# One block of tokens is normed, queried and chosen ahead of the others; the norms of the last two blocks stand behind the first products of fetched rows

## The reference

```python
o = jnp.concatenate([o_gdn, o_rwkv], axis=-1) @ w_out[layer]
x = x + gt1 * o[:, n_ctx:]
x = x + gt2 * peer_ffn(modulate(rms_norm(x, norm2_g[layer]), sh2, sc2), ...)

def peer_ffn(h, w_query, sub_keys, down, up):
    q = (h @ w_query).reshape(B, T, PEER_HEADS, 2, PEER_DKEY // 2)
    s = jnp.einsum('bthpd,hpkd->bthpk', q, sub_keys).astype(jnp.float32)
    s_top, i_top = lax.top_k(s, PEER_TOPK)
    ...
    best_s, pos = lax.top_k(cand_s, PEER_TOPK)
    idx = jnp.take_along_axis(cand_i, pos, axis=-1)
    gate = jax.nn.softmax(best_s, axis=-1)
    ...
        act = jax.nn.gelu(jnp.einsum('td,ted->te', h_blk, down[i_blk]), approximate=False)
        return jnp.einsum('te,ted->td', act * g_blk, up[i_blk])
```

## Time and profile before

| | us |
|---|---|
| median of 3 runs | 4005.07 (4001.75 to 4008.58) |
| the profiled execution's own time | 4012.65 |
| its span, first to last instruction | 4010.8 |
| TensorE busy in the span | 3541.0 (88%) |
| VectorE busy | 2607.9 (65%) |
| ScalarE busy | 1024.8 (26%) |
| GpSimd busy | 1212.8 (30%) |

### The profile page before, as it was taken

The page is one execution under the profiler, slowest core; times in us unless marked ns, Lnnn a source line. Parts: engine busy times, 40 slices in busy tenths (PEclk is TensorE's granted clock), DMA queues, the critical chain, the costliest instruction groups (busy, mean ns, idle before and its releaser), DMA issues. The chain is left out here.

```text
span 4010.8 us, 54734 instructions
## 1 busy us (share of the span) xinstructions
PE 3541.0 (88%) x21607; PEld 2096.7 (52%) x21607; DVE 2607.9 (65%) x4972; ACT 1024.8 (26%) x2744; POOL 1212.8 (30%) x1197
## 2 busy tenths in 40 slices
PE   7998899999987988777777777689999999999998
PEld 4556666888845544332233333355555444458863
DVE  4866535787656666776777675556666667547765
ACT  1432222444222323323333333330000012510000
POOL 1034301544211334333333334223232320014432
PEclk8999999999998999999999999999999999999999
DMA  4157620000028999999999999701112431012233
GB/s 173 42 211 244 229 76 1 11 3 3 3 95 296 402 416 420 420 421 420 420 420 421 420 421 420 305 23 46 60 63 95 167 131 64 1 42 85 85 135 137
DMA packets 184398, 786.68 MB, mean 196 GB/s; under 512 B 13574, under 2 KB 76305, under 8 KB 109136
## 3 DMA queue, kind: packets, MB, share of 16 engines
q0 software_dynamic: 77408, 550.32, 33.3%
q1 hardware_dynamic: 105584, 230.77, 16.4%
q10 hardware_dynamic: 1152, 2.10, 0.1%
HBM read 781.03 MB, written 2.10 MB: 195 GB/s over the span
## 5 line engine op out<-in xcount | busy, mean ns | idle before, releaser
L2584 PE MATMUL bank<-row,dg 128*128 128x512 f32 x1444 | 699.3, 625 | 207.6 <-ACT dg L2693 207.2
L2786 DVE CUSTOM_DVE_ANT_0 row<-row,bank 128x1024 f32<-128x1024 f32 x361 | 440.9, 1221 | 297.1 <-DMA row<-in_experts,idxs 276.9
L2584 PEld LDWEIGHTS bank<-row,dg 128*128 128x128 f32 x1444 | 275.4, 198 | 595.7 <-issue 582.8
L2852 POOL DMA_INDIRECT row<-in_experts,idxs x361 | 348.6, 966 | 627.3 <-PE bank L2584 565.7
L2584 PE MATMUL bank<-wring,dg 128*128 128x512 f32 x604 | 288.1, 610 | 71.2 <-ACT dg L2693 71.2
L104 PE MATMUL bank<-hT,wring 128*128 128x256 f32 (+1 forms) x864 | 285.1, 490 | 3.7 <-ACT sq L830 3.0
L3548 DVE TENSOR_TENSOR pad<-pad,bank 128x256 f32<-128x256 f32 (+2 forms) x396 | 154.1, 412 | 191.9 <-PE bank L104 184.6
L2684 ACT ACTIVATE act<-dots 128x2 f32<-128x2 f32 x256 | 52.0, 203 | 825.2 <-DVE dots L2786 825.2
L2786 DVE CUSTOM_DVE_ANT_0 wring<-wring,bank 128x1024 f32<-128x1024 f32 x151 | 184.5, 1222 | 111.3 <-DMA wring<-in_experts,idxs 103.3
L2584 PEld LDWEIGHTS bank<-wring,dg 128*128 128x128 f32 x604 | 112.8, 194 | 230.9 <-issue 223.8
L104 PEld LDWEIGHTS bank<-hT,wring 128*128 128x128 f32 x864 | 165.4, 192 | 118.8 <-issue 101.3
(11 more groups left out here) (605 smaller groups left out, 6591.6 us busy)
## 6 DMA issues: line engine op xcount, KB each, us to landing
wring<-in_ada_w SPq DMA_DIRECT2D x64, 1024.0 KB, 5.6
wring<-in_ffn_w_down SPq DMA_DIRECT2D x50, 1024.0 KB, 6.9
wring<-in_ffn_w_up SPq DMA_DIRECT2D x44, 1024.0 KB, 7.7
wring<-in_peer_w_query SPq DMA_DIRECT2D x16, 1024.0 KB, 10.9
wring<-in_w_in SPq DMA_DIRECT2D x7, 2048.0 KB, 8.3
wring<-in_ada_w SPq DMA_DIRECT2D x4, 2048.0 KB, 11.1
wring<-in_attn_w_qkv SPq DMA_DIRECT2D x3, 2048.0 KB, 7.9
row<-in_experts,idxs POOLq DMA_INDIRECT x361, 24.7
```

What stands on the lines that cost most here:

```text
L2584: ins = e.matmul(ks[half], self.dg[u % 4], self.places[self.slot[u]][:, 1024 + half * 512:1536 + half * 512], start=(x == 0), stop=(x == 127))
L2786: e.tensor_tensor_reduce(row, row, P.pairs[g % 2], 1.0, 0.0, MUL, ADD, self.dots[:, g % 2, x:x + 1]).then_inc(*V.up("pg_dot", j))
L2852: e.indirect_dma_start(self.places[r], None, P.i["experts"], bass.IndirectOffsetOnAxis(ap=idu[:, b, j % 128:j % 128 + 1], axis=0)).then_in ...
```

## The change

`Experts` loses its `super().pe(pe)` and the like, and what `Experts` did ahead of the 512 steps moves into `MixerOut`.

- TensorE: the keys are turned right behind block 2's turn; behind the products of blocks 3 and 2 come the turn of block 3's `h2`, queries 0 to 7 with their scores, then the four `out_pe` of blocks 1 and 0 (first the half f whose weights lie in ring slot 0, then the other, 1-f; here f = 1), then queries 8 to 15, the gate row, and the turns of `h2` of blocks 2, 1, 0.
- ScalarE: its work is put in the matching order. `weigh` of block 3 stands ahead of queries 8 to 15; the roots of blocks 2, 1, 0 stand among those queries.
- VectorE: `heads_dv` of block 0 behind `normed(3)`; the choice of block 3; `normed(1)` behind the dot of row 0, `normed(0)` behind that of row 1, the gate row behind that of row 2.
- SyncE: the first eight query tiles go through two places (where `sk` lay and where `ogdn` lay) where there were four; each waits for the tile two ahead of it.
- GpSimd: the first seven fetches wait for what lies in their places: `wfree` for j = 0 to 2, the queries of tile 6 for j = 3, `pq_rows` of block 0 (the end of `normed(0)`) for j = 4 to 6. `final_norm_g` is loaded ahead of j = 8.

```diff
@@ MixerOut.dv
             self.heads_dv(dv, b)
         self.added(dv, 3, 0)
         self.added(dv, 3, 1)
-        self.heads_dv(dv, 0)
         dv.wait_ge(*P.at("pq_scale"))
         e.tensor_scalar(self.Ar, self.Ar, 1.0, None, ADD).then_inc(*V.up())
-        self.added(dv, 2, 0)
-        self.added(dv, 2, 1)
...
         self.normed(dv, 3)
+        self.heads_dv(dv, 0)
+        self.added(dv, 2, 0)
+        self.added(dv, 2, 1)
+        choice, f = P.experts.choose(dv, 3, 0), self.first
+        take(choice, 10)
+        self.added(dv, 1, f)
+        take(choice, 2)
+        self.added(dv, 0, f)
+        take(choice, 1)
+        self.added(dv, 1, 1 - f)
+        for _ in choice:
+            pass
+        self.added(dv, 0, 1 - f)
         self.normed(dv, 2)
-        self.added(dv, 1, 0)
-        self.added(dv, 0, 0)
-        self.added(dv, 1, 1)
-        self.normed(dv, 1)
-        self.added(dv, 0, 1)
-        self.normed(dv, 0)
@@ MixerOut.ac
+        ac.wait_ge(*P.at("ro_y", 0))
+        for n in range(8):
+            x.query_ac(ac, 0, n)
+            if n:
+                x.scores_ac(ac, 0, n - 1)
+            if n == 3:
+                self.squares(ac, 2)
+        self.turned_ac(ac, 0, 1)
+        x.scores_ac(ac, 0, 7)
+        x.rows_ac(ac, 0)
+        x.weigh(ac, 3, 0)
+        self.squares(ac, 1)
+        for n in range(8, 16):
+            x.query_ac(ac, 0, n)
+            if n > 8:
+                x.scores_ac(ac, 0, n - 1)
+            if n == 10:
+                self.squares(ac, 0)
+                self.root(ac, 2)
+            if n == 12:
+                self.root(ac, 1)
+            if n == 14:
+                self.root(ac, 0)
+        x.scores_ac(ac, 0, 15)
+        for b in (2, 1, 0):
+            self.out_ac(ac, b)
@@ MixerOut.pe
+        self.out_pe(pe, ws, 2, 0)
+        self.heads_pe(pe, 1)
+        self.gate_pe(pe, 0)
+        self.out_pe(pe, ws, 2, 1)
+        P.cycle((2, 3, 4, 5))
+        self.rows_pe(pe, 3)
+        pe.wait_ge(*P.at("free", "pq_h", 3, 1))
+        pe.wait_ge(*P.at("free", "pq_keys", 3))
+        for n in range(8):
+            x.query_pe(pe, 0, n, 0, 8)
+            if n:
+                x.scores_pe(pe, 0, n - 1)
+        P.cycle((6, 7, 0, 1))
+        self.heads_pe(pe, 0)
+        k = P.own(pe, 2, "pq_s", 0, 7)
+        x.scores_pe(pe, 0, 7, k)
+        self.out_pe(pe, ws, 1, f)
+        self.out_pe(pe, ws, 0, f)
+        T_.mark("wfree", ws[f][0])
+        self.out_pe(pe, ws, 1, 1 - f)
+        self.out_pe(pe, ws, 0, 1 - f)
+        T_.mark("wfree", ws[1 - f][0])
+        P.cycle((2, 3, 6, 7))
+        for n in range(8, 16):
+            x.query_pe(pe, 0, n, 0, 8)
+            if n > 8:
+                x.scores_pe(pe, 0, n - 1)
+        x.scores_pe(pe, 0, 15)
+        mod_row(pe, P, T_, "pg_gate", lambda n: P.modT[0][:, 40 + n, 0:1])
         for b in (2, 1, 0):
             self.rows_pe(pe, b)
@@ Experts.dv
+            if j == 0:
+                P.rout.normed(dv, 1)
+            if j == 1:
+                P.rout.normed(dv, 0)
+            if j == 2:
+                keep_row(dv, P, V, "pg_gate", self.gt)
@@ Experts.po
-            elif r >= early - 2:
-                po.wait_ge(*P.at("query_w_free", 4 + r - (early - 2)))
+            elif r >= 4:
+                po.wait_ge(*P.at("pq_rows", 0))
+            elif r == 3:
+                po.wait_ge(*P.at("query_w_free", 6))
+            else:
+                po.wait_ge(*P.at("wfree", ws[f if r < 2 else 1 - f][0]))
```

More of the change, by code:

```diff
@@ L1669, in __init__ @@
         self.bon = P.mem("bon", 2048, 4, 4, 128)
+        self.ybase = P.top
         self.y = P.mem("y", 2048, 4, 8, 64)
@@ L2144, in __init__ @@
         assert P.top <= hbase + 27 * T
+        P.top = hbase + 27 * T
+        self.oT = [P.mem("oT", 2048, 4, NX)]
+        assert P.top <= rs.ybase
+        P.top = hbase + 11 * T + 4096
+        self.oT.append(P.mem("oT", 2048, 4, NX))
+        assert P.top <= hbase + 19 * T
         P.top = rs.big
@@ L2277, in ac @@
         A.mark("ro_bs")
+        x = P.experts
         for b in self.BLOCKS:
@@ L2296, in ac @@
             e.activation(self.skT[:, 4 * q:4 * q + 4, :], v4(P.ps("pq_keys", q)), ACT.Copy).then_inc(*A.up("free", "pq_keys", q))
-        self.out_ac(ac, 2)
-        self.squares(ac, 0)
-        self.root(ac, 0)
-        self.out_ac(ac, 1)
-        self.out_ac(ac, 0)
+        self.squares(ac, 3)
+        self.root(ac, 3)
+        self.turned_ac(ac, 1, 1)
+        self.root_ac(ac, 0)
+        self.out_ac(ac, 3)
+        ac.wait_ge(*P.at("ro_y", 0))
[24 more added lines that the diff above has]
+            self.out_ac(ac, b)
     def root_ac(self, ac, b):
@@ L2346, in pe @@
         ws = [P.weight("pe", 8, 512) for _ in range(2)]
+        x, f = P.experts, ws[0][0] % 2
+        self.first, self.ws = f, ws
         self.heads_pe(pe, 3)
@@ L2394, in out_pe @@
         pe.wait_ge(*P.at("free", "ro_T", b, 1))
-        mm(pe.e, k, [(self.oT[:, c, b * 128:(b + 1) * 128], wb[:, c, :]) for c in range(8)]).then_inc(*self.T.up("ro_o", half, b))
+        mm(pe.e, k, [(self.oT[c // 4][:, c % 4, b * 128:(b + 1) * 128], wb[:, c, :]) for c in range(8)]).then_inc(*self.T.up("ro_o", half, b))
     def rows_pe(self, pe, b):
@@ L2492, in __init__ @@
         quarter = [P.wring[:, n * 2048:(n + 1) * 2048] for n in range(4)]
-        self.wq = Tiles(P, "query_w", quarter, 8)
-        first += quarter[0:2]
+        P.top = P.obase
+        self.wq = Tiles(P, "query_w", quarter[2:4] + [first[0], P.mem("wq", 2048)], 8)
+        first = quarter[0:2] + [first[1], first[0]] + first[2:]
         self.places = first + old + quarter[2:4] + hq
@@ L2519, in place @@
     def place(self, n):
-        return n % 4 if n < 8 else 2 + n % 2
+        return 2 + n % 2 if n < 8 else n % 2
     def sy(self, sy):
@@ L2525, in sy @@
         wq = P.i["peer_w_query"][0].rearrange("(c p) n -> p c n", p=128)
-        P.begin(sy, "rout")
         for n in range(16):
-            after = None if n < 4 else n - 4 if n < 8 else 6 + n % 2 if n < 10 else n - 2
+            after = None if n < 2 or n in (8, 9) else n - 2
+            if n == 0:
+                sy.wait_ge(*P.at("pq_keys", 3))
+            if n == 1:
+                sy.wait_ge(*P.at("ro_T", 0, 0))
+            if n == 8:
+                sy.wait_ge(*P.at("wfree", P.rout.ws[1 - P.rout.first][0]))
             self.wq.load(sy, n, self.place(n), after, wq[:, :, n % 8 * 256:n % 8 * 256 + 256])
@@ L2536, in query_pe @@
         if c0 == 0:
+            if which and n == 0:
+                pe.wait_ge(*P.at("free", "pq_h", 0, 1))
             self.kq = P.bank(pe, "pq_q", which, n)
@@ L2545, in query_pe, with scores_pe @@
                 self.T.mark("query_w_free", w)
-    def scores_pe(self, pe, which, n):
+    def scores_pe(self, pe, which, n, k=None):
         P = self.P
-        k = P.bank(pe, "pq_s", which, n)
+        k = P.bank(pe, "pq_s", which, n) if k is None else k
         pe.wait_ge(*P.at("free", "pq_q", which, n))
@@ L2627, in ac @@
     def ac(self, ac):
-        super().ac(ac)
         P, e, A = self.P, ac.e, self.A
-        self.rows_ac(ac, 0)
-        for n in range(17):
-            if n < 16:
-                self.query_ac(ac, 0, n)
-            if n:
-                self.scores_ac(ac, 0, n - 1)
-        self.weigh(ac, 3, 0)
         rest = self.rest_ac(ac)
@@ L2834, in po @@
     def po(self, po):
-        super().po(po)
         P, e = self.P, po.e
+        ws, f = P.rout.ws, P.rout.first
         idu = self.idxs.bitcast(U32)
-        e.dma_start(self.fg, P.i["final_norm_g"].partition_broadcast(128)).then_inc(*self.Lf.up("final_norm"))
         early = len(self.places) - 6
```

48 lines of the change are left out of this document (10 added, 38 removed).

## The result

| | before | after |
|---|---|---|
| median of 7 runs each, us | 4008.58 (4001.75 to 4013.80) | 4019.57 (4014.74 to 4022.95) |
| the profiled execution's own time | 4012.65 | 4022.95 |
| its span | 4010.8 | 4020.9 |
| TensorE busy | 3541.0 | 3546.1 |
| VectorE busy | 2607.9 | 2609.1 |

The ratio is 1.0027, 95% interval 1.0017 to 1.0036: slower, by 11 us between the medians and by 10.3 between the profiled executions. That is small, but the interval leaves out 1. The choice of experts nevertheless ends 15 us earlier. The rows of after show where that is spent. The absolute times of these two executions can be compared: the turn of block 2, up to which nothing was moved, starts at 1137.93 in one and at 1137.82 in the other.

A forecast was written before the change was run, and what follows sets the result against it. TensorE was taken to set the pace for about the first 45 steps, so the end follows the first sum: `idxs` 15.2 earlier, first sum 8.8 later (1270.5 against 1261.65), 4005.07 + 8.8 = 4013.9 us, range +5 to +12.

The forecast's parts named there:

- Part 1: Start of block 3's choice on VectorE: one piece, waiting for the third `out_pe` and an `added`, at 1198.0 us.
- Part 2: End of the choice on VectorE: 37.4 us long, `idxs` at 1235.4, which is 15.2 earlier than 1250.59.
- Part 3: From `idxs` to first sum: late queries, norms and turns held behind the choice; first sum at 1270.5, 8.8 us later.
- queries 11 to 15 keep ahead of them, tile 7 (asked for at about 1244, landing at 1249.5) included: Late queries behind the choice: done early enough that VectorE's norms needn't wait for ScalarE's roots behind their copies.
- The opening: First to second sum on TensorE, at the lower clock: 5.75 us, as before.
- the shift stays to the end: From the first sum on, the steps are the same instructions, so the 8.8 us shift stays to the end.
- Rival A: Late queries not held during the choice: `normed(2)` 6.7 us earlier, total +2.1, 4007.2; chance 0.09.
- Rival B: Transfers bind from the first sums on, so fetch state counts: -1.2 us, 4003.9; chance 0.09.
- Rival C: The lead of the fetches carries, so the end moves with `idxs`: -15.2 us, 3989.9; chance 0.10.
- Rival D: Queries 0 to 7 on TensorE also run at the lower clock: +11.6 us on top, 4025.5; chance 0.06.
- Rival E: The documented drain at ScalarE's two table loads is real on this path: +2.8 us on top, 4016.7; chance 0.08.

The follow-up runs named there:

- e6_all: After with e1_take's iterated `take`, e2_free's banks, and the changes of e3_rows and e4_tiles together: median 3984.84 us against before's 4012.58, ratio 0.9939.
- e1_take: After with the three `take` calls iterated over, so the choice runs in pieces among the `added`: median 3994.86 us against before's 4012.58, ratio 0.9958.
- e4_tiles: After with query tiles 8 and 9 asked for only when tile 7 has been read: one run, span 4018.1 us where after has 4020.9.
- e2_free: After with late queries in banks 2, 3, 0, 7 and `weigh` behind the sixteenth score: median 4010.65 us against before's 4012.58, ratio 0.9998.
- e3_rows: After with the turns of `h2` of blocks 2, 1, 0 in banks 6, 7, 0, 1: median 4013.33 us against before's 4012.58, ratio 1.0003.
- e9_bank: After with only the late queries' banks altered to 2, 3, 0, 7, ScalarE's order kept: median 4014.34 us against before's 4007.94, ratio 1.0016.
- e5_hold: After with the first three fetches held until query tile 5 has been read: one run, span 4026.6 us where after has 4020.9.
- e11_early: e6_all with both norms ahead of dot 0, fetches held until tile 5 is read, tiles 8 and 9 requested behind tile 7: 3977.42 us against before's 4010.53, ratio 0.9921.
- e7_tile7: e6_all with fetches 1 and on held until query tile 7 has landed: ratio 0.9942 to before.

## Why the prediction was right, and where it was off

**The sum.** The forecast was +8.8; the third sum moved by 9.8, the profiled execution by 10.3, the medians by 11.0. The predicted 4013.9 is 5.7 below the measured 4019.57: 3.5 of it is the median of before, 4005.07 of three runs and 4008.58 of seven, and 2.2 the change.

**Part 1** held to a few tenths: query 0 at 1156.81 (1157.1), the products at 1175.60 (1175.6), the choice in one piece from 1197.74 (1198.0). That the start of the stretch lies where it did before (0.1 apart) is luck; others have it up to 5 off (1132.77 in e6_all). e1_take shows what hung on reading `take` right: two kernels that look alike are some 28 us apart by their ratios, 26.1 at the third sum.

**Part 2** held: the choice is 37.8 long (37.4) and `idxs` ends at 1235.58 (1235.4).

**Part 3** held in its mechanism and in its sum, with one term mis-sized. The wait for bank 6 ended at 1236.23 (1236.1), the table load was done at 1242.97 (1243.8), `normed(2)` at 1247.23 (1248.0), the gate row at 1264.78 (1264.1), the first sum started at 1271.16 (1270.5). The step that failed is "queries 11 to 15 keep ahead of them, tile 7 (asked for at about 1244, landing at 1249.5) included": tile 7 was asked for at 1242.14 and took 9.7, not 5.4, so root(0) was late and VectorE waited 2.59. I had sized the tile as if it were alone, with three fetches in flight. By e4_tiles, where root(0) no longer holds VectorE, the wait costs 1.9 at the third sum. It nearly vanishes in the total by luck: the queries ahead of `squares(0)` were 0.8 shorter than I had made them, and the norms and dots some 1 shorter. The opening was 0.3 longer (6.06 from first to second sum, against 5.75).

**That the shift stays to the end** is shown by thirteen traces.

**Rival A** has its price from e2_free: I gave 6.7 for the late queries let free, and it is 9.1. Up to the end of `normed(2)` it is 6.0 (65.6 behind the products, after 71.6); the wait for root(0) that I hadn't foreseen is gone too (0.27, after 2.59), dot 0 waits 0.5 for its fetch, and from the first sum to the third it is 1.3 shorter. **Rival B** didn't occur: VectorE's dots do wait for fetches (7.21 ahead of the one at 1280.73), but sums follow each other by 3.01 and TensorE is busy 100.00 of 100. **Rival C** is refuted by after, where `idxs` is 15.0 earlier and the end later, and by e1_take. **Rival D** didn't occur: queries 0 to 7 ran at full clock (granted 1.00 from 1156 to 1175), the products started on time. **Rival E** didn't either: the row behind a table load starts 0.02 and 0.01 after it (1242.99 and 1269.87), with the loads now on the path. ScalarE: Activation LUTs, section "What ACT_TABLE_LOAD costs", in the Trainium skill, has a drain of about 1.38 beside the load; this case's traces don't show it, behind the load or ahead of it (the row ahead of the first load ends at 1241.67, the load starts at 1241.69).

**Where the gain went.** 15.0 earlier `idxs`, and then four things behind it that used to lie under the choice or ahead of it: the queries held by a bank and by ScalarE's order (9.1 by e2_free), the turns that wait for the gate row (4.8 at the first sum by e3_rows; 7.8 at the third, with an opening at full clock), tile 7 (1.9 by e4_tiles), and the three norms themselves, about 4.4 each. The parts overlap and can't be added: the 9.1 and part of the 4.8 contain the wait for root(0), which is also what e4_tiles takes away. e2_free and e3_rows together were not run without the rest.

## What to carry to other kernels

When a step is pulled forward, list what was hidden under it and ask for each piece which bank, which buffer and which engine's order now ties it to the step's end: two lists of bank numbers cost some 5 each at the first sum (e9_bank, e3_rows) of the 15.0 that the reordering had gained. Look at whether a generator is iterated before believing the order in which a source reads. And transfers that one chain needs go ahead of those that a later one needs, all of them: a single tile or a single fetch favoured made the next one late, and the shortest way to the third sum was the whole row in the order of need (tiles 7 and 8, then the fetches, with tile 9 among them).

## What the runs showed of the hardware

A 1 MB tile of query weights took 5.4 to 5.8 to land when it was asked for ahead of the fetches, though others followed it (e5_hold, e9_bank, e11_early). It took 8.8 with one fetch issued ahead of it (and the end of tile 6, e7_tile7), 9.7 and 9.0 with three issued 3.7 to 6.7 ahead of it (after, e3_rows), and 14.3 and 15.7 with three issued 0.2 to 4.7 ahead of it (e1_take, e6_all); in these four a fourth fetch followed some 4 to 6 behind. In e6_all, from 1210 to 1214, with the tile and the fetches in flight, the two kinds of queue stand like this (packets, MB, share of the engines' time):

```profile
q0 software_dynamic: 195, 1.45, 87.6%
q1 hardware_dynamic: 187, 0.19, 13.7%
```

The fetches (q0) move about 7.4 KB a packet, the tile (q1) 1.0 KB. In these 4 us the tile moves 0.19 MB, where alone it moves 1.05 MB in 5.4: the fetches didn't share the bytes evenly with it, they nearly stopped it. DMA: Bandwidth & Descriptors, section "Queues, rings and completion order", in the Trainium skill, says that a DMA engine goes round between its queues and takes a whole packet from each. The trace agrees as far as the counts go, 195 packets to 187, if the profile's packets are the page's. That this is why the tile is late is argued and not shown, since no run here altered a packet size.

TensorE's clock at the first sum is not explained. In after, the sum took 3.75 (granted clock 0.50) behind pauses of 3.45 and 3.24; in e3_rows it took 1.96 (granted 1.00) behind one pause of 3.50, and the difference of about 3 us reached the third sum. But e6_all has the same 24 turns and the same pause, and stays at the lower clock (granted 0.53 from 1235.4 to 1239):

```profile
1229.15 2.78 PE L2460 MATMUL bank<-consts,h 128*128 128x128 f32 x24
1235.44 3.61 PE L2641 MATMUL bank<-wring,dg 128*128 128x512 f32 x4 [3.50 <-ACT dg L2742]
```

Of the thirteen traces only e3_rows has the first sum at full clock throughout. The count and length of the pauses right ahead of it don't decide it here.
